# Second half of the recurrence's output norm moved beside the first output tiles, with earlier requests for the output weights and rows

## What is computed

```
def rwkv_output(y, r, v, k, gl, p):      # y: forward + backward recurrence, 8 heads of 64
    y = (y - mean(y, head)) / sqrt(var(y, head) + 64e-5)     # per position and head
    y = y * ln_x_w + ln_x_b
    bonus = sum(r * k * r_k, head) * v
    return (y + bonus) * (sigmoid(gl) @ g2)

out = concat([y_r, y_d], -1) @ w_out      # 512 recurrent columns, 512 of attention
x = x + gt1 * rmsnorm(out, g_post_mix)
h = modulate(rmsnorm(x, g_pre_ffn), sh2, sc2)
u = dwconv(h @ w_up, ffn_conv)            # the next stage
```

## Time and profile before

| | us |
|---|---|
| median of 3 runs | 3891.55 (3891.1 to 3891.93) |
| the profiled execution, its own time | 3886.74 |
| its span, first to last instruction | 3885.0 |
| PE busy in it | 3590.0 (92%) |
| DVE busy | 1754.6 (45%) |
| ACT busy | 962.5 (25%) |
| chain that ended last: PE, DVE, ACT, DMA | 84%, 9%, 4%, 2% |

### The profile page before, as it was taken

One profiled execution on the slowest core, in us unless ns is written; L12 is line 12 of the kernel. 1 busy time (PEld: TensorE's weight loads), 2 busy tenths in 40 slices (PEclk: granted clock), 3 DMA queues, 4 the chain that ended last, 5 costly groups with the idle time before them and its releaser, 6 DMA issues.

```text
span 3885.0 us, 63673 instructions
## 1 busy us (share of the span) xinstructions
PE 3590.0 (92%) x28989; PEld 2243.8 (58%) x28989; DVE 1754.6 (45%) x2533; ACT 962.5 (25%) x1900; POOL 47.3 (1%) x114
## 2 busy tenths in 40 slices
PE   7998879989999996789999998999899799999988
PEld 3546655559988986344444443444566444777753
DVE  2048852245556555332222220022999663544524
ACT  3015620135455553121111110000011301233320
POOL 2000000000000000000000000000000000000000
PEclk9999989989999998899999999999999899999999
DMA  6011110000000000331011101113011112000021
GB/s 221 22 43 66 66 65 7 28 6 17 4 17 4 4 4 5 114 103 36 30 44 44 43 22 38 44 54 103 22 33 33 43 60 67 22 27 28 1 76 65
DMA packets 108143, 168.08 MB, mean 43 GB/s; under 512 B 5203, under 2 KB 66386, under 8 KB 107234
## 3 DMA queue, kind: packets, MB, share of 16 engines
q1 hardware_dynamic: 99890, 134.77, 10.4%
q10 hardware_dynamic: 7984, 29.25, 2.1%
HBM read 142.51 MB, written 21.50 MB: 42 GB/s over the span
## 4 chain that ended last, share of the span: by engine, by line
PE 84%; DVE 9%; ACT 4%; DMA 2%; issue 1%; SPq 0%; ACTq 0%; DVEq 0%
PE psum_all L66 83%; ACT sbuf_all L75 3%; DVE sbuf_all L102 3%; DVE sbuf_all L94 3%; DVE sbuf_all L84 2%; PE psum_all L69 1%; ACT L75 1%; DMA sbuf_all<-in_w_mod 1%; DMA sbuf_all<-in_w_out 1%; DVE sbuf_all L91 0%; DVE sbuf_all L108 0%; DMA sbuf_all<-in_gla_w_out 0%; DVE sbuf_all L90 0%; DMA sbuf_all<-in_w_up 0%; DMA sbuf_all<-in_w_down 0%
## 5 line engine op out<-in xcount | busy, mean ns | idle before, releaser
L66 PE MATMUL psum_all<-sbuf_all 64*64 64x64 f32 (+10 forms) x28218 | 3484.0, 308 | 227.6 <-ACT sbuf_all L75 58.1
L66 PEld LDWEIGHTS psum_all<-sbuf_all 64*64 64x64 f32 (+5 forms) x28218 | 2152.5, 153 | 1537.4 <-issue 1101.5
L75 ACT ACTIVATE sbuf_all<-psum_all 128x512 f32<-128x512 f32 (+7 forms) x969 | 434.6, 468 | 1569.0 <-PE psum_all L66 1441.7
L94 DVE SCALAR_TENSOR_TENSOR sbuf_all<-sbuf_all 128x1040 f32<-128x1040 f32 (+8 forms) x571 | 624.0, 1094 | 24.8 <-PE psum_all L66 4.5
L75 ACT ACTIVATE sbuf_all<-sbuf_all 128x64 f32<-128x64 f32 (+12 forms) x449 | 259.9, 589 | 952.8 <-DVE sbuf_all L78 394.8
L84 DVE TENSOR_TENSOR sbuf_all<-sbuf_all 128x640 f32<-128x640 f32 (+10 forms) x497 | 403.9, 833 | 187.0 <-ACT sbuf_all L75 147.7
L78 DVE COPY sbuf_all<-psum_all 128x256 f32<-128x256 f32 (+5 forms) x137 | 71.1, 526 | 540.5 <-PE psum_all L66 526.4
L91 DVE TENSOR_SCALAR sbuf_all<-sbuf_all 128x1024 f32<-128x1024 f32 (+9 forms) x131 | 76.5, 589 | 470.3 <-ACT sbuf_all L75 467.7
L75 ACT ACTIVATE sbuf_all<-psum_all,sbuf_all 128x1280 f32<-128x1280 f32 (+5 forms) x212 | 164.3, 781 | 351.4 <-PE psum_all L66 323.2
L108 DVE COPY_PREDICATED sbuf_all<-sbuf_all,psum_all 128x256 f32<-128x256 int32 (+2 forms) x296 | 145.5, 493 | 159.3 <-PE psum_all L66 154.5
L69 PE MATMUL psum_all<-sbuf_all 128*128 128x128 f32 (+2 forms) x771 | 115.0, 294 | 56.2 <-DVE sbuf_all L90 27.0
(11 more groups left out here) (19 smaller groups left out, 125.8 us busy)
## 6 DMA issues: line engine op xcount, KB each, us to landing
sbuf_all<-in_w_mod SPq DMA_DIRECT2D x12, 2048.0 KB, 8.2
sbuf_all<-in_w_up SPq DMA_DIRECT2D x22, 1024.0 KB, 7.7
sbuf_all<-in_w_in SPq DMA_DIRECT2D x6, 2048.0 KB, 7.8
x_spill<-sbuf_all SPq DMA_DIRECT2D x16, 512.0 KB, 2.9
sbuf_all<-in_w_down SPq DMA_DIRECT2D x4, 2048.0 KB, 7.6
sbuf_all<-in_conv_w_in SPq DMA_DIRECT2D x16, 512.0 KB, 6.3
sbuf_all<-in_gla_w_in SPq DMA_DIRECT2D x8, 1024.0 KB, 5.2
sbuf_all<-in_x ACTq DMA_DIRECT2D x2, 2048.0 KB, 19.9
```

The lines of the kernel that those rows point to most:

```text
L66: return self.e.matmul(out, lhsT, rhs, start=start, stop=stop, skip_group_check=True)
L75: return self.e.activation(out, in_, func, bias=bias, scale=scale, **kw)
L94: return self.e.scalar_tensor_tensor(out, a, s, b, op0, op1) if self.e is not None else Unissued()
```

## The change

The output norm is cut by positions. `scanout_norm(half)` does for 2048 columns what the whole norm did for 4096; `scanout_turn(half)` and `scanout_gated(half)` are the turn on PE and the gating on DVE; `scanout_squares(half)` is ACT's part. The scanout stage keeps half 0 up to its turn. DVE in mix now does the gain row, gates half 0, norms half 1, and gates half 1 between its tiles 0 and 1. PE does the turn of half 1 between its tiles 1 and 2. ACT does the gain row and the squares of half 1 before it asks for x. The waits for `K.scanout.ends()` at the start of mix are gone; each engine waits for the signal it needs. SP asks for `K.ydT2` as soon as scan has ended, and for `w_out` when the last gate matmul and POOL's bonus have ended. The norm's gain, shift, statistics and bonus tiles move in memory, out of the place of `K.ydT2`.

```diff
 def scanout_memory(K):
     K.yrT = sb.take(4 * SEQ, j=4)
+    at = K.rwkv_keep + 200
+    sb.at = at + 8192
     K.lnw, K.lnb = sb.take(256), sb.take(256)
...
     K.bv = sb.take(4096, i=16, j=4)
-    at = K.rwkv_keep + 200
...
-def scanout_vector(K, ve):
-    Q = K.scanout
+def y_half(half):
+    return slice(32 * half, 32 * half + 32)
+
+def scanout_norm(K, ve, half):
+    Q, g, n = K.scanout, y_half(half), slice(8 * half, 8 * half + 8)
     V = Q.v
-    y, mean, var = K.y_heads, K.y_mean, K.y_var
+    y, sq, mean, var = K.y_heads[:, g], K.y_sq[:, g], K.y_mean[:, g], K.y_var[:, g]
...
-    ve.tt(y, y, spread(mean), ALU.subtract).then_inc(*V.tick("centred"))
-    ve.wait_ge(*Q.s.by("squares"))
+    ve.tt(y, y, spread(mean), ALU.subtract).then_inc(*V.tick("centred", half))
+    ve.wait_ge(*Q.s.by("squares", half))
...
     ve.wait_ge(*Q.g.by("bonus"))
-    for n in range(0, 16, 8):
-        ve.wait_ge(*V.now())
-        part = K.yacc[:, n:n + 8]
-        ve.tt(part, part, K.bv[:, n:n + 8], ALU.add).then_inc(*V.tick("normed", n // 8))
+    ve.wait_ge(*V.now())
+    ve.tt(K.yacc[:, n], K.yacc[:, n], K.bv[:, n], ALU.add).then_inc(*V.tick("normed", half))
+
+def scanout_gated(K, ve, half):
+    Q, cols = K.scanout, slice(half * 512, (half + 1) * 512)
+    for j in range(4):
+        ve.wait_ge(*Q.t.by("y_turned", half, j))
+        ve.wait_ge(*Q.s.by("gate", half, j))
+        ve.tt(K.yrT[:, j, cols], K.bank.view("y_turned", half, j), K.gateT[:, j, cols], ALU.mult).then_inc(*Q.v.tick("gated", half))
+        K.bank.end(("y_turned", half, j), Q.v.now())
+
+def scanout_vector(K, ve):
+    for s in K.scan.ends():
+        ve.wait_ge(*s)
+    scanout_norm(K, ve, 0)
...
 def mix_tensor(K, te):
     M = K.mix
-    for s in K.scanout.ends():
-        te.wait_ge(*s)
     gate_row_tensor(K, te, M, "row1", K.mix_diag)
     te.wait_ge(*K.dma("load_yd").final())
...
     for i in range(NT):
+        if i == 2:
+            scanout_turn(K, te, 1)
+        te.wait_ge(*K.scanout.v.by("gated", i // 4))
         for n, w in enumerate(halves):
...
 def mix_vector(K, ve):
-    for s in K.scanout.ends():
-        ve.wait_ge(*s)
+    ve.wait_ge(*K.scanout.t.by("gate", 1, 3))
     gate_row_vector(K, ve, M, "row1", K.mix_diag, K.mod[:, 16:24], K.col["g_post_mix"])
...
+    scanout_gated(K, ve, 0)
+    scanout_norm(K, ve, 1)
     for i in range(NT):
+        if i == 1:
+            scanout_gated(K, ve, 1)
...
 def mix_scalar(K, se):
-    for s in (*K.scanout.ends(), K.dma("spill_yd").final()):
-        se.wait_ge(*s)
-    se.dma_start(K.ydT2, K.yd_dram).then_inc(*K.dma("load_yd").tick())
+    gate_row_scalar(K, se, M, "row1", K.row1)
+    scanout_squares(K, se, 1)
     for i in range(3):
         load(i)
-    gate_row_scalar(K, se, M, "row1", K.row1)
...
 def mix_sync(K, sy):
-    for s in K.scanout.ends():
+    for s in (*K.scan.ends(), K.dma("spill_yd").final()):
         sy.wait_ge(*s)
+    sy.dma_start(K.ydT2, K.yd_dram).then_inc(*K.dma("load_yd").tick())
+    sy.wait_ge(*K.scanout.t.by("gate", 1, 3))
+    sy.wait_ge(*K.scanout.g.by("bonus"))
     for n in range(2):
         load_block(K, sy, ("out", n), K.io["w_out"][0], n * 512, 512)
```

More of the change, by code:

```diff
@@ L1814, in scanout_pool @@
               ALU.mult).then_inc(*Q.g.tick("bonus"))
-def scanout_vector(K, ve):
-    Q = K.scanout
+def y_half(half):
+    return slice(32 * half, 32 * half + 32)
+def scanout_norm(K, ve, half):
+    Q, g, n = K.scanout, y_half(half), slice(8 * half, 8 * half + 8)
     V = Q.v
-    for s in K.scan.ends():
-        ve.wait_ge(*s)
-    y, mean, var = K.y_heads, K.y_mean, K.y_var
-    yacc = K.yacc.rearrange("p n j f -> p n (j f)")
-    spread = lambda x: x.unsqueeze(2).broadcast_to([P, 64, HEAD])
-    row = lambda x: x.unsqueeze(1).broadcast_to([P, 16, 256])
+    y, sq, mean, var = K.y_heads[:, g], K.y_sq[:, g], K.y_mean[:, g], K.y_var[:, g]
+    yacc = K.yacc[:, n].rearrange("p n j f -> p n (j f)")
+    spread = lambda x: x.unsqueeze(2).broadcast_to([P, 32, HEAD])
+    row = lambda x: x.unsqueeze(1).broadcast_to([P, 8, 256])
     ve.reduce(mean, y, ALU.add).then_inc(*V.tick())
@@ L1829, in scanout_vector @@
     ve.wait_ge(*V.now())
-    ve.tt(y, y, spread(mean), ALU.subtract).then_inc(*V.tick("centred"))
-    ve.wait_ge(*Q.s.by("squares"))
-    ve.reduce(var, K.y_sq, ALU.add).then_inc(*V.tick())
+    ve.tt(y, y, spread(mean), ALU.subtract).then_inc(*V.tick("centred", half))
+    ve.wait_ge(*Q.s.by("squares", half))
+    ve.reduce(var, sq, ALU.add).then_inc(*V.tick())
     ve.wait_ge(*V.now())
-    ve.ts(var, var, 1.0 / HEAD, ALU.mult, 64e-5, ALU.add).then_inc(*V.tick("variance"))
-    ve.wait_ge(*Q.s.by("root"))
+    ve.ts(var, var, 1.0 / HEAD, ALU.mult, 64e-5, ALU.add).then_inc(*V.tick("variance", half))
+    ve.wait_ge(*Q.s.by("root", half))
     ve.recip(var, var).then_inc(*V.tick())
@@ L1872, in scanout_scalar, with scanout_squares @@
             K.bank.end(("gate", half, j), Q.s.now())
[L1873 to L1876, removed]
+    scanout_squares(K, se, 0)
+def scanout_squares(K, se, half):
+    Q, g = K.scanout, y_half(half)
+    se.wait_ge(*Q.v.by("centred", half))
+    se.activation(K.y_sq[:, g], K.y_heads[:, g], ACT.Square).then_inc(*Q.s.tick("squares", half))
+    se.wait_ge(*Q.v.by("variance", half))
+    se.activation(K.y_var[:, g], K.y_var[:, g], ACT.Sqrt).then_inc(*Q.s.tick("root", half))
 def scanout_tensor(K, te):
@@ L1888, in scanout_tensor, with scanout_turn @@
                       K.gl[0:GATE, half * 512:(half + 1) * 512]).then_inc(*Q.t.tick("gate", half, j))
[L1889 to L1896, removed]
+    scanout_turn(K, te, 0)
+def scanout_turn(K, te, half):
+    Q = K.scanout
+    te.wait_ge(*Q.v.by("normed", half))
+    for j in range(4):
+        bank = open_bank(K, te, "y_turned", half, j)
+        for n in range(8):
+            for rows in HALVES:
+                done = te.matmul(bank[rows, n * 64:(n + 1) * 64], K.yacc[rows, 8 * half + n, j, :], K.half_ident[rows, :])
+        done.then_inc(*Q.t.tick("y_turned", half, j))
 def mix_memory(K):
```

## The result

| | before | changed |
|---|---|---|
| median, four runs each | 3891.32 us (3889.72 to 3891.93) | 3855.9 us (3853.96 to 3860.13) |
| ratio, 95% interval | 1 | 0.9911 (0.9894 to 0.9928) |
| profiled execution, its own time | 3886.74 | 3853.96 |
| its span | 3885.0 | 3852.1 |

The changed kernel is 35.4 us faster by the medians, 0.9%; the forecast was 33.5.

A forecast was written before the change was run, and what follows sets the result against it. From norm to first output product, DVE, ACT and the w_out transfer, not PE, were taken as the bound, 71.7 us. 14.5 + 22.7 - 3.7 = 33.5 us saved, 3891.55 - 33.5 = 3858.0 us, range 3853.0 to 3862.0.

The forecast's parts named there:

- Step 1: Output norm to its last addition: norming one half instead of both ends at 1540.4 instead of 1554.87, saving 14.5 us.
- Step 2: From the turn to the first product: w_out's transfer is hidden, 11.9 us instead of 34.6, saving 22.7 us.
- Step 3: Turn of half 1 between output tiles 1 and 2, at full clock: 3.7 us given back, PE not waiting for DVE.
- The clock: PE's first output products: forecast case, chance 0.50, has the clock fall after the turn, as before, with 2.6 us lost.
- the rival, at 0.27: PE's clock stays up from turn into first products: saving 36.1 us, time 3855.4 us; chance 0.27.
- Transfer is the bound anyway: w_out holds the first product until the same time as before: only 0 to 3 us saved; chance 0.03.
- DVE's second norm holds the tiles: Norm of half 1 delays the output tiles, taking 71 us instead of 19: slower, 3900 us; chance 0.02.
- losses at the seam: Subtraction awaits POOL's fourth, row matmul at half clock, or w_out late: together 2 to 5 us, about 3861.5; chance 0.17.
- Whole time: Whole kernel: 33.5 us saved, median 3858.0 us; for the profiled execution, span 3851.5 and time 3853.2.

The follow-up runs named there:

- POOL after centring: Changed kernel, POOL starting its bonus only once DVE has centred half 0; first reduce to first transpose 101.6 us, changed kernel 101.4.
- POOL and ACT cleared: Changed kernel, POOL copying factors and forming bonus by halves after the squares, ACT squaring half 0 after two gate copies, w_out awaiting only POOL's copy; stretch 100.3 us.
- extra matmuls: Changed kernel with eight unread matmuls on PE from the variance of half 0, ahead of its turn; stretch 100.4 us, changed kernel 101.4.
- halves in front: Changed kernel, half 1 normed, turned and gated ahead of the first output tile, not beside tiles 0 and 1; stretch 123.8 us, changed kernel 101.4.
- the early requests alone: Kernel before with only SP's early requests and the new memory places, norm whole; stretch 120.1 us, before 136.8; 3877.17 us in all.
- late requests: Changed kernel, SP waiting for the gating of half 0 before asking for attention rows and w_out; stretch 124.3 us, changed kernel 101.4.
- gap: Changed kernel with four DVE memsets ahead of the gating of half 0, lengthening PE's idle time; stretch 107.0 us, changed kernel 101.4.

## Why the prediction was right, point by point

- **Step 1** (14.5 us): right to 0.1. The half is normed at 22.61 us after the reduce; the working gave 22.64. The subtraction got in ahead of POOL's fourth instruction (it ended 7.98 us after the reduce, I had 8.1), and POOL ended 2 us later than before, 9.66 us instead of 7.60. The rule of the Trainium skill ("SBUF — State Buffer", "Who interferes with whom") fits: mean and subtraction were held, the reduce beside POOL took 2.29 us as the other did. But the prediction let the hold count as 3.1 us of the path, and the run with POOL later shows that it wasn't: ACT's gate copies would have held the squares to within 0.3 us of the same moment. I had noted that ACT is free only at that time, and did not draw the conclusion.
- **Step 2** (22.7 us): the first product came 34.53 us after the reduce; the 1552.3 of the prediction is 34.54. `w_out` landed 12 us ahead of it. The transfer rate was well taken: 12.3 us forecast, from 1529.58 to 1542 measured. Turn and row took 7.63 us where I had 7.35, gain row and gatings 4.3 where I had 4.5.
- **Step 3** (3.7 us given back): right in kind. 59.25 us for tiles 0 to 3 with the second turn are 54.9 (four tiles at 13.73, full clock) and 4.3 for the turn, 0.6 more than I had. That turn is 64 matmuls in 128 records; the prediction calls the records matmuls, which changes no time. DVE's second norm took 19.2 us where I had 19.1, and PE never waited for it.
- **The clock** is the term that was off, and it is the forecast's choice of case that failed here: the sum had the first products at the half clock (2.6 us); the rival, at 0.27, had it stay up. In the changed kernel's two profiles it stayed. That is 2.6 us off a stretch of 103.3 by my terms; the second turn took 0.6 back, and 101.4 remained. So the saving of 35.4 us lies nearer to the rival's 36.1 than to the forecast's 33.5. That 33.5 came close owes something to luck, since the clock was a matter of 2.6 us and I had it on the wrong side. The rows I argued from (the fall between 1566 and 1568) were evidence for one of two outcomes that both occur with such gaps: in the runs with POOL and ACT cleared and with extra matmuls it fell. The page "TensorE: Matmul & The Clock Gate" of the Trainium skill, section "Part 1: The HAM clock gate (the "warmup" mystery)", warns that the point of transition varies from run to run; this case agrees (behind the same start of the turn, 22.6 us after the reduce, the grant rose at 28.4 in one run and 25.4 in another).
- **Rivals.** "Transfer is the bound anyway" holds only if it is asked for late: then PE waits 23.96 us for it. "DVE's second norm holds the tiles" didn't happen, with 9 us to spare. Of the "losses at the seam" none happened: the subtraction got in ahead of POOL's fourth instruction, the row matmul took two records at the full clock, and `w_out` was early.
- **Whole time.** 3855.9 against 3858.0. The profiled execution (3853.96) is 0.8 us above the 3853.2 worked out for it, although the stretch is 1.9 us better than my terms: its first reduce started 2.0 us later than in the profile of before, and the rest behind the transposes took 0.5 us more (2230.97 against 2230.43). The last 0.1 to 0.2 us are rounding and the step from span to own time.

## What to carry to other kernels

Where a chain of DVE, ACT and a transfer stands between two PE-bound stages, the gain is in what can be put beside the next stage's first tiles, not in cutting the work: halves in front of the tiles were worth nothing over the early requests alone, halves beside them 18.7 us. A wait that the chain of waits shows is worth removing only down to the next engine that would have held the same instruction; look at that engine's queue first. With drifts of some us elsewhere in the program, measure a change by the stretch between two fixed events of the trace, and try small edits together as well as alone.

## What was not expected

- The whole time of the changed kernel spreads by 6 us (3853.96 to 3860.13). In its two profiled executions (3853.96 and 3854.30) the stretch repeats within 0.1 us; the slowest ones weren't profiled, so where their time goes isn't shown. The first reduce alone wandered by 8.8 us over thirteen profiles. Where ahead of it that arises was not followed.
- ACT's four small reads of `ln_x_w` and `ln_x_b` (64 KB each) took 2.7 us to landing before and 7.8 and 7.6 us behind the early read of the attention rows, and ACT's issue of the last two 1.60 us instead of 1.30. They are needed 15 us after the reduce, so it cost nothing here.
- The clock's two courses. Eight profiles have a turn, a gap of 1.6 us, the row matmul and a second gap. In four of them the grant rose 28.4 us or more after the first reduce, near the turn's end (changed kernel twice, POOL after centring, halves in front); in the first three it was still up when the products began at about 34.6, and in the fourth, where PE idled on, it fell at 35.5. In the other four it rose by 25.4 (late requests, gap, POOL and ACT cleared) or at 18.2 (extra matmuls), and in all of these it fell between 31.8 and 32.2, in or just behind the second gap. No profile of the changed kernel itself took the second course. An estimate from the gap run: it would give 1.4 us in the turn, and by the runs with POOL and ACT cleared and with extra matmuls take 1.7 in the products. What decides between the courses stays open.
